# Two plain tiles in place of three at the head of each feed-forward stage, and a third slot whose products are split

## The reference, cut to what matters

```python
def swiglu_ffn(x, w_in, w_out):
    gate, up = jnp.split(x @ w_in, 2, axis=-1)
    return (jax.nn.silu(gate) * up) @ w_out

def trunk(x):
    for l in range(DEPTH):                       # DEPTH = 2
        x = layer_norm(ALPHA * x + 0.5 * swiglu_ffn(x, ffn_a_w_in[l], ffn_a_w_out[l]), ln_g[l, 0], ln_b[l, 0])
        mix = even_mixer(x, ...) if l % 2 == 0 else odd_mixer(x, ...)
        x = layer_norm(ALPHA * x + mix, ln_g[l, 1], ln_b[l, 1])
        x = layer_norm(ALPHA * x + 0.5 * swiglu_ffn(x, ffn_b_w_in[l], ffn_b_w_out[l]), ln_g[l, 2], ln_b[l, 2])
    return x
```

## Time and profile before

| what | value |
|---|---|
| runs | 2399.04, 2399.17, 2400.26 us; median 2399.17 |
| the profiled execution | 2400.26 us, its span 2398.4 us |
| TensorE busy | 2348.8 us, 98% |
| VectorE busy | 1715.6 us, 72% |
| ScalarE busy | 1155.9 us, 48% |
| GpSimd busy | 589.9 us, 25% |
| mean granted clock of TensorE | 0.997 |

### The profile page before, as it was taken

The page is one execution under the profiler, slowest core; times in us unless marked ns, Lnnn a source line. Parts: engine busy times, 40 slices in busy tenths (PEclk is TensorE's granted clock), DMA queues, the critical chain, the costliest instruction groups (busy, mean ns, idle before and its releaser), DMA issues.

```text
span 2398.4 us, 40127 instructions
## 1 busy us (share of the span) xinstructions
PE 2348.8 (98%) x15868; PEld 2054.4 (86%) x15868; DVE 1715.6 (72%) x2232; ACT 1155.9 (48%) x1661; POOL 589.9 (25%) x310
## 2 busy tenths in 40 slices
PE   9999999999999999999999999999999999999998
PEld 8989977777778989988989988878787888998996
DVE  7828767998769818769728675798988547863857
ACT  5525537885446525535525434455454334542543
POOL 2040034001232040141030144333333334013013
PEclk9999999999999999999999999999999999999999
DMA  5333322232123333223333323222222222323322
GB/s 170 99 108 103 105 90 62 84 95 71 53 79 106 95 108 106 90 87 107 94 100 109 99 79 102 80 72 80 80 80 71 71 79 88 106 91 110 108 84 84
DMA packets 64847, 220.96 MB, mean 92 GB/s; under 512 B 11194, under 2 KB 15802, under 8 KB 64542
## 3 DMA queue, kind: packets, MB, share of 16 engines
q1 hardware_dynamic: 64670, 218.47, 29.2%
...
## 4 chain that ended last, share of the span: by engine, by line
PE 78%; DVE 11%; issue 7%; ACT 2%; POOL 1%; DMA 0%; POOLq 0%; SPq 0%; ACTq 0%; DVEq 0%
PE ps L709 12%; PE ps L710 12%; PE ps L711 12%; PE ps L889 9%; PE ps L888 9%; PE ps L887 9%; PE ps L697 3%; PE ps L691 3%; PE ps L692 3%; DVE sb_x L2346 1%; PE ps L1307 1%; DVE sb_Up L2639 1%; DVE sb_wl L2480 1%; DVE sb_x L2338 1%; DVE sb_x L2350 1%
## 5 line engine op out<-in xcount | busy, mean ns | idle before, releaser
L601 POOL TENSOR_TENSOR sb_low<-sb_src,sb_hi 128x1408 fp32r<-128x1408 f32 x64 | 206.0, 3221 | 1110.6 <-ACT sb_hi L1482 1110.6
L601 POOL TENSOR_TENSOR sb_wl<-sb_raw,sb_wh 128x1024 fp32r<-128x1024 f32 x118 | 294.4, 2496 | 533.4 <-ACT sb_wh L1482 509.6
L2157 DVE TENSOR_TENSOR sb_low<-sb_src,sb_hi 128x1024 fp32r<-128x1024 f32 (+1 forms) x304 | 329.6, 1091 | 74.8 <-ACT sb_hi L1546 63.9
L1546 ACT ACTIVATE sb_hi<-sb_src 128x1024 fp32r<-128x1024 f32 (+1 forms) x304 | 285.8, 946 | 186.4 <-PE ps L889 100.4
L887 PE MATMUL ps<-sb_tt,sb_hi 128*128 128x256 f32 x1216 | 344.1, 283 | 0.0
L888 PE MATMUL ps<-sb_tt,sb_low 128*128 128x256 f32 x1216 | 344.1, 283 | 0.0
L889 PE MATMUL ps<-sb_tt,sb_hi 128*128 128x256 f32 x1216 | 344.1, 283 | 0.0
L1482 ACT ACTIVATE sb_wh<-sb_raw 128x1024 fp32r<-128x1024 f32 x143 | 151.3, 1058 | 257.5 <-PE ps L711 221.8
L888 PE MATMUL ps<-sb_xh,sb_low 128*128 128x256 f32 x912 | 258.1, 283 | 0.0
L889 PE MATMUL ps<-sb_xl,sb_hi 128*128 128x256 f32 x912 | 258.1, 283 | 0.0
L887 PE MATMUL ps<-sb_xh,sb_hi 128*128 128x256 f32 x912 | 258.1, 283 | 0.0
...
## 6 DMA issues: line engine op xcount, KB each, us to landing
...
sb_raw<-w_od SPq DMA_DIRECT2D x80, 512.0 KB, 3.6
sb_raw<-w_ev SPq DMA_DIRECT2D x40, 512.0 KB, 3.6
...
sb_src<-w_in SPq DMA_DIRECT2D x16, 512.0 KB, 3.6
sb_raw<-w_evo SPq DMA_DIRECT2D x8, 512.0 KB, 3.6
sb_raw<-w_odo SPq DMA_DIRECT2D x8, 512.0 KB, 3.6
```

Source lines behind the costliest of these rows:

```text
L601: pool.tensor_tensor(sl.wl[:, 0:n], sl.raw[:, 0:n], sl.wh[:, 0:n].bitcast(F32), ALU.subtract).then_inc(lo_done, 1)
L1546: act.activation(hi[:, lo_:hi_at, :], groups(i)[g], ACT.Copy).then_inc(hi_s[g], 1)
L2157: dve.tensor_tensor(low[:, a_:b_, :], groups(i)[g], hi[:, a_:b_, :].bitcast(F32), ALU.subtract).then_inc(lo_s[g], 1)
```

## The change

PLAIN becomes 2. A feed-forward stage has four plain slots and 20 tiles in block pairs, in chunks of 9 and 11. The first two tiles' banks, the raw buffers of slots 2 and 3 (`raw_h`) and the loads' waits follow from that.

The third slot of each stage but the first is split: `third` puts 16 of its products with sequence 0 (256 columns) inside `pair`, and `third_rest` does the rest behind it. For that its split moves on ScalarE to the place between the norm's two sequences, and slot 1's split moves ahead of the table load; GpSimd's low of slot 1 moves ahead of its lows of x where the stage before is a feed-forward stage.

The work for the first block pair is put in another order on ScalarE and VectorE: T3, T2, T1, T4, with T1 and T4 after the weight groups 0 to 2, and the product of plain tile 1 (`plain_glu(1)`), for which p1 of pair 1 now waits, behind `up_second(0)` and s2 of pair 1.

```diff
-PLAIN = 3
+PLAIN = 2
...
+A_BANK = (6, 4)
...
                 if more:
-                    low_of_x(st + 1, 0, LOW_POOL[:1])
-                    lo(KD, Slot(stages[st + 1][1], 0, 2, 1))
-                    low_of_x(st + 1, 0, LOW_POOL[1:])
+                    first = int(kind != "ffn")
+                    low_of_x(st + 1, 0, LOW_POOL[:first])
+                    if first:
+                        pool.wait_ge(w_used, stages[st + 1][1] + 2)
+                    lo(KD, next_slot(st, 1))
+                    low_of_x(st + 1, 0, LOW_POOL[first:])
...
                 for k in (1, 2, 3, 5, 6):
                     low(0, k)
+                if between:
+                    between[0]()
                 for k in LOW_DVE:
                     low(0, k)
+                if between:
+                    between[1]()
...
                 def p1(i):
                     if i == 1:
-                        pe.wait_ge(glu_done, FT * fi + 2 + 3)
+                        pe.wait_ge(glu_done, FT * fi + 1 + 3)
...
+            def third(bank, sl):
+                out = ps[:, bank, part(0)]
+                def high():
+                    pe.wait_ge(hi_done, sl.n + 3)
+                    for k in range(KD):
+                        pe.matmul(out, sl.wh[:, k * P:(k + 1) * P], xh[:, k, part(0)], start=k == 0, stop=False)
+                def low():
+                    for k in LOW_POOL + LOW_DVE:
+                        pe.matmul(out, sl.wh[:, k * P:(k + 1) * P], xl[:, k, part(0)], start=False, stop=False)
+                return high, low
+            def third_rest(bank, sl):
+                out = ps[:, bank, part(1)]
+                for k in range(KD):
+                    w_h = sl.wh[:, k * P:(k + 1) * P]
+                    pe.matmul(out, w_h, xh[:, k, part(1)], start=False, stop=False)
+                    pe.matmul(out, w_h, xl[:, k, part(1)], start=False, stop=False)
+                pe.wait_ge(lo_done, sl.n + 3)
+                for k in range(KD):
+                    mm = pe.matmul(ps[:, bank, :], sl.wl[:, k * P:(k + 1) * P], xh[:, k, :], start=False, stop=k == KD - 1)
...
-                    pair((0, 1), (fs(0), fs(1)), st, rest)
-                for f, bank in ((2, 2), (3, 3), (4, 6), (5, 7)):
-                    of_x_late(bank, fs(f))
+                    pair((0, 1), (fs(0), fs(1)), st, rest, third(4, fs(2)))
+                    third_rest(4, fs(2))
+                for f, bank in ((2, 4), (3, 5)):
+                    if f > 2 or st == 0:
+                        of_x_late(bank, fs(f))
...
-                pair((1, 0), (sl(ev_u(0)), sl(ev_m(0))), st, rest)
-                of_x_late(2, sl(ev_g(0)))
+                third_slot = mix_slot(n0, ev_g(0))
+                pair((1, 0), (sl(ev_u(0)), sl(ev_m(0))), st, rest, third(6, third_slot))
+                third_rest(6, third_slot)
...
-                hi_t(T1)
                 hi_t(T3)
                 silu_plain(0, 0)
                 hi_t(T2)
-                hi_t(T4)
-                split(KD, fs(4))
-                silu_plain(1, 2)
-                split(KD, fs(5))
-                seven(*CHUNKS[0], OUT0 - 1, OUT0, (2, 6))
+                seven(*CHUNKS[0], OUT0 - 1, OUT0, (1, 4), (T1, T4))
...
                 squares(KD - 2)
+                if nxt:
+                    split(KD, next_slot(ln, 1), next_slot(ln, 1).n)
...
                 rstd(0)
-                if more:
-                    split(KD, Slot(stages[ln + 1][1], 0, 2, 1))
                 for k in range(KD):
                     tile(0, k)
...
+                if more:
+                    split(KD, next_slot(ln, 2), stages[ln + 1][1] + 2)
                 for k in range(KD):
                     tile(1, k)
...
+                    if i0 == 0:
+                        split_low(2, 0)
+                        t_sums(T1)
+                        s4(0)
+                        t_sums(T4)
+                        t_low(T1)
+                        split_low(0, 1)
+                        split_low(3, 0)
+                        t_low(T4)
+                        s13(1)
+                        up_second(0)
+                        s2(1)
+                        plain_glu(1, 5)
+                        split_low(1, 1)
+                        plain_split(1)
...
                 lo(2)
-                dve.tensor_tensor(tsum[T1][:], b11, b12, ALU.subtract).then_inc(t_sum, 1)
-                dve.tensor_tensor(tsum[T3][:], b22, b12, ALU.subtract).then_inc(t_sum, 1)
+                t_sums(T3, T2)
                 lo(3)
...
-                t_low(T1)
                 t_low(T3)
-                plain(0, 1)
+                plain_glu(0, 1)
+                plain_split(0)
                 t_low(T2)
-                t_low(T4)
-                lo(4)
-                plain(1, 3)
                 s13(0)
                 s2(0)
-                lo(5)
-                seven(*CHUNKS[0], (2, 7))
+                seven(*CHUNKS[0])
```

More of the change, by code:

```diff
@@ L165, in build @@
     GROUP = {1: 0, 6: 1, 7: 1, 2: 2, 5: 2, 4: 3, 3: 3}
-    T1, T3, T2, T4 = range(4)
+    T3, T2, T1, T4 = range(4)
     ma = [free]
@@ L354, in build @@
         stages_ffn = [n0 for kind, n0, _ in stages if kind == "ffn"]
+        after_mixers = [n0 for st, (kind, n0, _) in enumerate(stages) if kind == "ffn" and st and kinds[st - 1] != "ffn"]
         MIX_EVEN, MIX_ODD = NH + KD, HG + NH
@@ L422, in build, with mix_slot, next_slot @@
         OUT_HOME = home(0, 8)
+        IN_HOME = ((raw_h[:, 0, :], hi_c, low_c), (raw_h[:, 1, :], hi_c[:, 4 * T:], low_c[:, 4 * T:]))
+        FIRST_HOME = tuple((raw[:, p, :], (wh[:, 0, :], hi_c[:, 2 * T:4 * T])[p], wl[:, p, :]) for p in range(2))
         def ffn_slot(n0, f):
-            where = None if f < 2 else home(0, 2) if f < 4 else home(8, 10) if f < OUT0 else OUT_HOME
+            if f < 2:
+                where = FIRST_HOME if n0 in after_mixers else None
+            else:
+                where = IN_HOME if f < OUT0 else OUT_HOME
             return Slot(n0, f // 2, 2, f % 2, where)
+        THIRD_HOME = ((raw[:, 0, :], hi_c[:, 0:2 * T], hi_c[:, 2 * T:4 * T]),)
+        def mix_slot(n0, j):
+            return Slot(n0, 0, 2, j, THIRD_HOME if j == 2 else None)
+        def next_slot(st, j):
+            kind, n0, _ = stages[st + 1]
+            return ffn_slot(n0, j) if kind == "ffn" else mix_slot(n0, j)
+        A_BANK = (6, 4)
         def tile_of(i):
@@ L499, in out @@
                     load(slot_of(a["w_out"], 2 * KD * fi + f - OUT0), KH, fs(f))
-                for f in range(begun, 4):
-                    plain(f)
-                for f in (4, 5):
-                    sync.wait_ge(w_used, fs(f - 4).n + 3)
+                for f in range(begun, OUT0):
+                    if f == 2:
+                        sync.wait_ge(w_used, n0 + 2)
                     plain(f)
@@ L725, in of_x_late, with pair @@
                 proj_late(bank, KD, sl, x_h, x_l)
-            def pair(banks, sls, n, rest=None):
+            def pair(banks, sls, n, rest=None, between=None):
                 first, second = sls
@@ L739, in mul @@
                 def mul(z, q, w, x_, k, start=False, stop=False):
-                    return pe.matmul(out[z][:, part(q)], w[:, sls[z].par, k * P:(k + 1) * P], x_[:, k, part(q)],
+                    w_z = sls[z].wh if w is wh else sls[z].wl
+                    return pe.matmul(out[z][:, part(q)], w_z[:, k * P:(k + 1) * P], x_[:, k, part(q)],
                                      start=start, stop=stop)
@@ L819, in first_pair @@
                 pe.wait_ge(zeros_done, 1)
-                for _ in range(5):
-                    pe.matmul(ps[:, 7, part(0)], lt[:, 0, 0:P], lt[:, 0, part(0)], start=True, stop=True)
+                for b in (7, 7, 7, 2, 3):
+                    pe.matmul(ps[:, b, part(1)], lt[:, 0, 0:P], lt[:, 0, part(0)], start=True, stop=True)
                 pe.wait_ge(first_hi, 1)
@@ L878, in product @@
                     pe.wait_ge(t_lo, 4 * fi + t_ + 1)
-                out = ps[:, bank, 0:L]
+                out = ps[:, bank, part(i % 2) if bank < 4 else part(0)]
                 for k in range(KQ4):
@@ L1244, in sl @@
                     return Slot(n0, 0, 2, j)
-                pair((0, 1), (sl(0), sl(1)), st, rest)
-                of_x_late(2, sl(2))
+                pair((0, 1), (sl(0), sl(1)), st, rest, third(6, mix_slot(n0, 2)))
+                third_rest(6, mix_slot(n0, 2))
                 for m in range(3, 5):
@@ L1518, in hi_t, with seven @@
                     act.activation(tt[:, 0, n, :, :], tsum[n][:], ACT.Copy).then_inc(t_hi, 1)
-                def seven(i0, i1, last_slot, outs_, plain=None):
+                def seven(i0, i1, last_slot, outs_, plain=None, t_parts=()):
                     def split_hi(g, i):
@@ L1586, in seven @@
                         copy1(i)
+                        if i == i0 and t_parts:
+                            hi_t(t_parts[0])
                         if i < i1 - 1:
@@ L1591, in seven @@
```

(15 more changed lines are left out.)

80 lines of the change are left out of this document (45 added, 35 removed).

## The result

The changed kernel takes 2414.76 us (median of six runs, 2413.46 to 2418.67) against 2400.06 for the kernel before: a ratio of 1.0063 with a 95% interval of 1.0053 to 1.0073, or 14.7 us more. The forecast was 2410.4, with 2399 to 2418 as its range, and slower with a chance of 0.76. Direction and range held; the size was 11.3 and is 14.7.

The account below looks back on a forecast made before the run. TensorE bounds the kernel before, VectorE the ramps after. Stages 0 to 5 give +4.2, -1.5, +4.5, +2.7, -1.9 and +3.3, in all +11.3 us: 2410.4 against the median, range 2399 to 2418.

Parts of the forecast that it names:

- Plain to blocks: In four stages, two plain slots (10.90 us) go and a block pair (10.04) comes: -0.86 us of PE each.
- VectorE's list: Feed-forward ramp: steps from slot 2's low to plain_glu(1) take 23.1 us, plus 0.9 of waits.
- p1(1)'s delay: Feed-forward ramp: 5.7 us of idle PE, some at p5(0), the rest at p1(1); the stage's first half ends 3.1 later.
- The third slot: 16 of its products hide in the first pair, 3.73 us in place of 5.45 behind it: -1.72 at five transitions.
- turns into waiting: In feed-forward stages VectorE bounds the ramp, so neither the -0.86 nor the -1.72 us shortens the stage.
- 2.2 us of room: In the first pair, PE needs 5.75 of 7.52 us from 1087.05 on; about 2.2 us were taken as free.
- The normalization: GpSimd finishes its lows of x earlier, so VectorE's chain is 0.45 us shorter in stages 1, 3 and 4.
- Rival A: TensorE stays the bound in the ramps and every gain counts: -11.3 us, 2388; chance 0.10.
- The moved split ahead of stage 2: Even mixer to stage 2: slot 1's split waits for its weights' load, +1.4 us on VectorE's chain.
- The likeliest sum: All stages: +11.3 us without a clock loss, forecast 2405 to 2415; chance 0.58.
- rival C: Clock falls in four ramps after the new idle, 2 us lost in each: 2418.5; chance 0.18.
- the sign that the prediction itself names for C: The granted clock in the ramp drops below 1.00.

Follow-up runs that it names:

- the filled kernel: The changed kernel with idle TensorE filled by 12 matmuls of 256 columns ahead of p5(0) and 22 ahead of p1(1): 2411.06 us.
- the last kernel: Against the kernel with three plain tiles and the third slot split, GpSimd's low of slot 1 put back behind its first low of x: 2390.75 us.

## Why the prediction was right, and where its size was off

- **Plain to blocks, -0.86 a stage, turned into waiting: right.** The first chunk has 63 products for 56, and the ramp waits. Stage 2 is the clean case: +3.2 against +3.1, and so are stages 2, 3 and 5 of the filled kernel.
- **VectorE's list: right.** Forecast 23.1 us of steps and 0.9 of waits, measured 24.0 from 1098.10 to 1122.10 with 0.73 of waits. p1(1)'s delay was priced at 5.7 and is 12.64 - 7.17 = 5.5; in stage 0 it is 43.14 - 30.93 - 7.17 = 5.0, as worked out. Pricing the whole list of the other engine, and testing the prices on the list of before, placed the delay to 0.2 us. Of its two parts the sizes were less exact: about 2 and 3 to 4 us were forecast, 1.7 to 1.8 and 2.0 to 2.9 stand in the rows, and p5(0) waits for ScalarE's copy and not, as the prediction has it, for T1's low.
- **The third slot: right in the price, wrong in that it "turns into waiting" in an ffn stage.** 16 products hide in the pair; the kernel without the split shows 1.1 of the 1.72 us reaching p1(1). The sum had it right all the same, since p1(1) was placed by VectorE's list, not by adding. (The 2.2 us of room that the prediction finds in the pair count the wait of 0.43 ahead of 1087.05; from there on 7.52 - 5.75 is 1.8.) Over the whole kernel the split gives 9.75 us with three plain tiles and 5.5 with two.
- **The normalization: the size right, the reason in part.** The pair ends 0.45 earlier in stages 3 and 4, as forecast, and VectorE's two lows take 0.76 for 1.26. The prediction names two things: ScalarE's split leaves its place, and GpSimd is done with its lows of x when VectorE's come. Both are in the last kernel's rows. GpSimd's own order, which I had put it down to for the last kernel, is not the cause: with it put back the two lows still take 0.75. (Rival A's sum counts the 0.45 as 0.9 for its three stages, where 1.35 is meant; it would be 2387 or 2388 either way.)
- **The moved split ahead of stage 2: mis-sized.** Forecast +1.4. The load of slot 1 took 3.6 us here, not the 4.8 of the earlier trace rows, and the mean's copy came 0.24 later relative to ScalarE's squares:

```profile
717.96 0.62 ACT L1690 ACTIVATE sb_lt<-sb_x 128x512 f32<-128x512 f32 x1
718.93 1.06 ACT L1545 ACTIVATE sb_hi<-sb_raw 128x1024 fp32r<-128x1024 f32 x1 [0.36 <-DMA sb_raw<-w_in]
...
721.63 0.37 ACT L1755 ACTIVATE sb_lt<-ps 128x256 f32<-128x256 f32 x1
```

  The mechanism holds where the load is late: in the profiled execution of the kernel with three plain tiles and no split third slot it took 5.0 us, ScalarE waited 1.74 for it, and the even mixer's stretch is 356.52 against 354.93, +1.6.

```profile
718.03 1.06 ACT L1545 ACTIVATE sb_hi<-sb_raw 128x1024 fp32r<-128x1024 f32 x1 [1.74 <-DMA sb_raw<-w_in]
```

  So one load's landing in one execution was too thin a row for a term of the sum. It makes most of the -1.4 that the even mixer's stretch is below its forecast.
- **The clock: a rival that came true in part.** The likeliest sum took none of it, rival C 2 us in each of four ramps. It fell in three ramps of four, which is the sign that the prediction itself names for C, and the kernel with its waits filled puts the price at 3.7 us by the medians; a sum without this term puts it at nothing. With 0.18 C had too small a chance: the rows bounded the new idle only by waits of 0.49 and 6.54 us. The Trainium skill, page "TensorE: Matmul & The Clock Gate", section "Why this matters for your kernels", warns of pauses between bursts of matmuls. The trace agrees in stages 0, 3 and 5 and not in stage 2, where the clock read 1.00 after the same waits.

So the sum was 3.4 us short by the medians, and the clock is worth 3.7. With the clock up in the ramps, in the filled kernel, the difference from before is 11.0 us for the 11.3 forecast. Part of that closeness is luck: in its profiled execution the even mixer's stretch is 1.6 under its forecast (353.69, +0.35 forecast on 354.93), and 0.4 up to stage 0's second chunk (187.95) and 0.8 from there to the pair end of stage 1 (201.78) make most of it up. What lies behind these two no run shows; the second varies from 200.60 to 201.78 among the five kernels with two plain tiles.
